# Two pairs of heads at a time in the gated attention layers of a fused model block

## The chip, the cores and the metric

One core of one Trainium2 chip runs the whole program as one launch. The metric is device time in microseconds (us). TensorE (PE in the rows) does matmuls and transposes, VectorE (DVE), ScalarE (ACT) and GpSimd (POOL) work on what it leaves in PSUM and SBUF, SyncE (SP) issues the weight loads. The granted TensorE clock was 1.000 of full speed (2.4 GHz) over the profiled execution.

## What is computed

The reference takes `x` of 512 tokens by 1024 in fp32 through four attention layers and then a mixed layer with a feed-forward part. The four layers are, in this order:

```
for i in range(DEPTH):                 # DEPTH = 4
    kind = i % 3
    y = _mla_branch(...) if kind == 0 else _swa_branch(...) if kind == 1 else _fox_branch(...)
    x = _layernorm(DEEPNORM_ALPHA * x + y, ln_g[i], ln_b[i])
```

Each has 16 heads with values of 64 columns and ends in `(o * silu(gate)) @ w_out`. In short:

- MLA (layers 0 and 3): latent queries (384) and keys and values (256), each head's query and key has 64 plain and 32 rotated columns, `softmax(q k^T * scale)` over all earlier keys, then times `v`.
- SWA (layer 1): 16 query heads over 4 key heads, a window of 128 keys, a slope times the distance subtracted from the scores, and a sink in the softmax's sum.
- FOX (layer 2): dense causal attention with `cum[q] - cum[k]` added to the scores, where `cum` is the running sum of the log of a forget gate.

The fifth layer is no gated attention: it joins a short convolution, a pooling mixer (means over 2, 4, 8, 16 tokens, each group times a matrix) and two attentions with a relative bias, one of them over selected keys; a feed-forward part of 2816 and a small gated embedding follow.

## The kernel before, in words

**Numbers.** Every fp32 matrix product is done as three fp32r matmuls: an operand is split in a high part (rounded to fp32r) and a low part (the rest), and the products high x high, high x low, low x high are added in PSUM (`three`, `columns`). ACT makes the high part, DVE (for weights GpSimd) the low part. Value products and transposes are plain fp32 matmuls.

**Weights** come in units of up to 128x1024 elements in the order of `plan_units`, which is also the order in which PE uses them. SP loads a unit into one of three raw buffers, ACT rounds it (`split`, three units ahead, called by `advance`), GpSimd makes the low part, and PE reads one of four places of a ring. A place comes free when PE is done with the unit in it.

**PSUM** has eight banks of 512 fp32 columns. Projections and value products ("groups") alternate between banks 6 and 7: PE waits for `bank_free` of the group before the last (`begin`), and the reader that takes a group's last part frees it (`stored`). Scores use banks 0 to 5 (0 to 3 in the window layer), transposed probabilities banks 4 and 5.

**A pair** is two heads that share a 128-row tile. `pair_attention` is written once for each of PE, ACT and DVE, and each is a list of steps in a fixed order; the semaphores tie the lists together. The steps for a pair are:

- PE `scores(i, ch)` (line 735; 748 with FOX's extra rows, 758 with the rotated part): 64-row matmuls, the two heads side by side. The 512 queries are taken in 128-query blocks t with 128 to 512 keys, put together in three chunks (two in SWA), each chunk in its own two banks.
- DVE `maxima(i, ch)` (L2274): adds mask or bias, writes the scores to SBUF (`SBP`, two buffers for even and odd pairs), takes the row maximum, and frees the chunk (`ps_free`). In SWA the bias of a pair is made first (L2265). After the last chunk come the negative maxima (L2284, L2286; semaphore `pnb`).
- ACT `exps(i, x)` for head x (L1551): the exponential in place, with its sum (`pexp`).
- DVE `norm(i, x)` (L2303): times the reciprocal of the sum (`pnorm`).
- PE `turn(i, x, ch)` (L776): 128x128 transposes, in chunks of up to four, three chunks a head (two in SWA), to a bank that ACT empties into `PTP` (`turned`, L1577, semaphore `pt_free`). A dense head has 10 transposes, a window head 7.
- PE `mix(i)` (L791): values times transposed probabilities, 64-column matmuls, the two heads side by side in one bank of the projections.
- DVE `mixed(i)` (L2318): times half the gate, into `otmp`; ACT `gated_high(i)` (L1601) rounds it, DVE `gated_low(i)` (L2327) makes the low part (semaphore `po_lo`). There is one `otmp`: a pair's product waits for the low part of the pair before it.

**The order before.** The loop runs i from -2 to 7. In each turn PE does the projections that later pairs need (`fill`) and weaves into them, every third matmul, the transposes of pair i; then it does all scores of pair i+2, then the value product of pair i. The last pair's transposes are woven into the first rows of the output projection (`out_ahead`). In MLA `fill` is a rope tile, a query tile, the keys and values of two pairs, and a gate; in SWA a query tile and a gate; in FOX a query tile, a key tile, a gate, and after every third pair the values (`pair_values`) of two pairs more. A query or key or gate tile of SWA and FOX is 24 matmuls of 512 columns. ACT's `fill` rounds the tiles, takes tanh of the gates, and issues small DMAs: `rel_rows` in SWA, `aug_rows` and `rope_tables` in FOX.

Two places outside the attention loops matter. Ahead of FOX, DVE sets constant rows (L2636 to L2645, eight of them of two rows each) and adds the forget bias (L2649, four small additions); ACT and DVE finish the log of the gate, and PE makes the running sum as matmuls (L1173). In the fifth layer, GpSimd makes the window sums (`window_sums`, L2875 to L2884) that PE multiplies in `pooled` (L1228).

## Time and profile before

| | us |
|---|---|
| median of 3 runs | 1663.32 (1662.29 to 1670.09) |
| the profiled execution | 1662.11 |
| its span, first to last instruction | 1660.1 |
| PE busy | 1630.5 (98%) |
| DVE busy | 777.2 (47%) |
| ACT busy | 768.8 (46%) |
| POOL busy | 653.8 (39%) |

Busy shares are shares of the span. A matmul's busy time begins when it starts and ends when its last column has left the array, so the next one starts while the last is still busy; what a matmul costs in a stream is the distance from its start to the next one's start. The idle time in brackets in the rows below is time in which the engine ran nothing, with the instruction that ended it.

### The profile page before, as it was taken

The numbers are of one execution on the slowest core, as the hardware profiler recorded it, in microseconds if no ns is written. First come the engines' busy times: TensorE is split into PE (matmuls) and PEld (weight loads), VectorE is DVE, ScalarE is ACT, GpSimd is POOL, SyncE is SP. The second block draws the span as 40 slices with busy tenths as digits, with TensorE's granted clock in tenths as the row PEclk, the third lists the DMA queues.
The fourth block names the chain that finished last, engine by engine and source line by source line (L and its number), as shares of the span: only waits on it lengthen the run. The fifth ranks groups of instructions, "written<-read, shape, count | busy, mean of one in ns | idle before, by whom it ended". The sixth has DMA issues, their size and how long they took to land.

```text
span 1660.1 us, 24632 instructions
## 1 busy us (share of the span) xinstructions
PE 1630.5 (98%) x9349; PEld 1334.3 (80%) x9349; DVE 777.2 (47%) x2048; ACT 768.8 (46%) x1565; POOL 653.8 (39%) x551
## 2 busy tenths in 40 slices
PE   8999999999999999999999999999999999999998
PEld 8777789887888787888787788777788888888877
DVE  3767635566453434445777646887151111001152
ACT  4466724656244545533567634428653323212252
POOL 5323234332343424235422244882235444444423
PEclk9999999999999999999999999999999999999999
DMA  6323144333542323144222156331243333333312
GB/s 174 71 46 79 47 165 132 79 72 69 156 135 77 90 53 95 58 165 107 61 66 58 52 179 183 92 89 52 84 145 102 96 95 102 101 90 94 123 63 89
DMA packets 216048, 161.19 MB, mean 97 GB/s; under 512 B 53755, under 2 KB 197147, under 8 KB 215932
## 3 DMA queue, kind: packets, MB, share of 16 engines
q1 hardware_dynamic: 205904, 130.21, 27.9%
q10 hardware_dynamic: 9804, 29.38, 5.9%
q8 instruction: 75, 1.23, 0.3%
q14 instruction: 41, 0.34, 0.1%
q0 software_dynamic: 224, 0.03, 0.1%
HBM read 148.32 MB, written 11.14 MB: 96 GB/s over the span
## 4 chain that ended last, share of the span: by engine, by line
PE 82%; DVE 9%; ACT 6%; issue 2%; POOL 1%; DMA 1%; DVEq 0%; SPq 0%; ACTq 0%; POOLq 0%
PE banks L543 40%; PE banks L494 8%; PE banks L496 7%; PE banks L495 7%; PE banks L776 5%; PE banks L791 4%; PE banks L735 4%; PE banks L625 4%; ACT AB L1551 2%; ACT w_hi L1421 1%; DVE banks L2414 1%; PE banks L758 1%; DVE banks L2403 1%; DVE AB L2416 1%; ACT G L1681 1%
## 5 line engine op out<-in xcount | busy, mean ns | idle before, releaser
L2920 POOL TENSOR_TENSOR w_lo<-w_raw,w_hi 128x512 fp32r<-128x512 f32 (+2 forms) x506 | 613.1, 1239 | 976.9 <-ACT w_hi L1421 965.6
L1421 ACT ACTIVATE w_hi<-w_raw 128x1024 fp32r<-128x1024 f32 (+4 forms) x254 | 249.2, 994 | 169.8 <-PE banks L496 103.0
L543 PE MATMUL banks<-XTh,w_hi 128*128 128x512 f32 (+5 forms) x1216 | 290.7, 375 | 3.8 <-DVE XTl L2376 1.4
L543 PE MATMUL banks<-XTl,w_hi 128*128 128x512 f32 (+5 forms) x1216 | 279.5, 368 | 0.0
L543 PE MATMUL banks<-XTh,w_lo 128*128 128x512 f32 (+5 forms) x1216 | 271.1, 365 | 0.0
L543 PEld LDWEIGHTS banks<-XTh,w_lo 128*128 128x128 f32 (+2 forms) x1216 | 211.0, 187 | 38.1
L543 PEld LDWEIGHTS banks<-XTh,w_hi 128*128 128x128 f32 (+2 forms) x1216 | 203.7, 188 | 43.6 <-issue 8.0
L543 PEld LDWEIGHTS banks<-XTl,w_hi 128*128 128x128 f32 (+2 forms) x1216 | 208.5, 187 | 35.4
L494 PE MATMUL banks<-w_hi,OTh 128*128 128x512 f32 (+1 forms) x448 | 172.7, 386 | 0.6 <-DVE QKl L2126 0.5
L496 PE MATMUL banks<-w_hi,OTl 128*128 128x512 f32 (+1 forms) x448 | 167.9, 375 | 0.0
L495 PE MATMUL banks<-w_lo,OTh 128*128 128x512 f32 (+1 forms) x448 | 167.9, 375 | 0.0
L1577 ACT ACTIVATE AB<-banks 128x512 f32<-128x512 f32 (+1 forms) x200 | 101.6, 529 | 140.0 <-PE banks L776 139.6
L1551 ACT ACTIVATE AB<-AB,nb 128x256 f32<-128x256 f32 (+3 forms) x288 | 152.5, 533 | 1.3 <-DVE nb L2286 1.2
L2303 DVE TENSOR_SCALAR_CACHE_REDUCE AB<-AB,ri 128x256 f32<-128x256 f32 (+3 forms) x256 | 118.2, 518 | 2.3
L2811 DVE TENSOR_TENSOR otmp<-banks,AB 128x512 f32<-128x512 f32 x22 | 15.2, 691 | 189.2 <-PE banks L543 189.2
L776 PE MATMUL banks<-ident,AB 128*128 128x128 f32 x672 | 100.7, 274 | 2.2 <-DVE mx L2274 1.1
L494 PEld LDWEIGHTS banks<-w_hi,OTh 128*128 128x128 f32 x448 | 84.3, 188 | 19.3 <-issue 2.4
L776 PEld LDWEIGHTS banks<-ident,AB 128*128 128x128 f32 x672 | 80.6, 140 | 23.6 <-issue 8.1
L2126 DVE TENSOR_TENSOR QKl<-banks,QKh 128x512 fp32r<-128x512 f32 (+2 forms) x80 | 54.6, 683 | 93.6 <-ACT QKh L1450 92.0
L496 PEld LDWEIGHTS banks<-w_hi,OTl 128*128 128x128 f32 x448 | 84.3, 188 | 15.4
L495 PEld LDWEIGHTS banks<-w_lo,OTh 128*128 128x128 f32 x448 | 84.5, 189 | 13.3
L2274 DVE CUSTOM_DVE_ANT_0 AB<-banks,zmask 128x256 f32<-128x256 f32 (+1 forms) x192 | 82.2, 485 | 0.4
(230 smaller groups left out, 2208.4 us busy)
## 6 DMA issues: line engine op xcount, KB each, us to landing
w_raw<-in_w_gate_up_dram SPq DMA_DIRECT2D x44, 512.0 KB, 3.8
w_raw<-in_fox_w_in_dram SPq DMA_DIRECT2D x30, 512.0 KB, 4.1
w_raw<-in_mla_w_in_dram SPq DMA_DIRECT2D x26, 512.0 KB, 5.0
w_raw<-in_w_in_dram SPq DMA_DIRECT2D x24, 512.0 KB, 3.9
w_raw<-in_w_down_dram SPq DMA_DIRECT2D x22, 512.0 KB, 3.5
w_raw<-in_swa_w_in_dram SPq DMA_DIRECT2D x20, 512.0 KB, 4.5
w_raw<-in_mla_w_out_dram SPq DMA_DIRECT2D x16, 512.0 KB, 3.9
x_spill<-AB ACTq DMA_DIRECT2D x16, 512.0 KB, 2.7
```

The lines of the kernel that those rows point to most:

```text
L494: nc.tensor.matmul(o, ah, bh, start=first, stop=False, skip_group_check=True)
L495: nc.tensor.matmul(o, ah, bl, start=False, stop=False, skip_group_check=True)
L496: return nc.tensor.matmul(o, al, bh, start=False, stop=last, skip_group_check=True)
L543: mm = nc.tensor.matmul(o, wt[:, k, :], xt[:, k, lo:hi], start=first and n == 0 and k == 0, stop=last and n == 2 and k == nk - 1, skip_gro ...
L625: mm = nc.tensor.matmul(o[:, 256 * (t % 2):256 * (t % 2) + 256], xt[:, k, ts], parts[k // 4][low][:, k % 4, :], start=n == 0 and k == 0, s ...
L776: mm = nc.tensor.transpose(bank[4 + c.tch % 2][:, o:o + P], SBP[a % 2][x][:, col:col + P], ident[:, :])
L1421: nc.scalar.activation(view(w_hi, u, RING), view(w_raw, u, RAW), ACT.Copy).then_inc(hi_done, 1)
L1551: ins = nc.scalar.activation(sc, sc, ACT.Exp, bias=nb[:, b, n0 + t:n0 + t + 1], scale=pr.scale, accum_out=rs[:, b, n0 + t:n0 + t + 1])
L1577: nc.scalar.activation(PTP[x][:, pr.pt[js[0]]:pr.pt[js[0]] + width], bank[4 + c.tch % 2][:, 0:width], ACT.Copy).then_inc(pt_free, 1)
L2274: ins = nc.vector.tensor_tensor_reduce(pr.score(b, x, t), o, pr.bias(t, x), 1.0, -3e38, ALU.add, ALU.max, mx[:, b, 4 * x + t:4 * x + t + 1])
L2303: ins = nc.vector.tensor_scalar(pr.score(b, x, t), pr.score(b, x, t), ri[:, b, 4 * x + t:4 * x + t + 1], None, ALU.mult, ALU.add, accum_ou ...
L2920: ins = pool.tensor_tensor(low[at], raw[at], high[at].bitcast(F32), ALU.subtract)
```

## The change

The four gated attention layers run two pairs at a time (`grouped`, which takes the place of `late`); the fifth layer's pairs keep their loop. For PE, a group s does: the projections for pairs 2s+2 and 2s+3 in one piece (`fill(s)`), all transposes of pairs 2s and 2s+1 (`block`), both value products, then all scores of pairs 2s+2 and 2s+3. Scores of pairs 0 and 1 come first. In the last group the transposes stay woven, two chunks at a time, into the first rows of the output projection (`last_block`, with `each=True` giving more points for it). Nothing is woven into projections any more.

```diff
+        TURN_BANKS = [4, 5, 0, 1, 2, 3]
+        def turn_bank(m, grouped, last):
+            return bank[TURN_BANKS[m % 6] if grouped and not last else 4 + m % 2]
+        def turned_to(pair, x, grouped):
+            return SBP[0][x] if grouped and pair % 2 else PTP[x]
...
+                def block(s):
+                    block_at[0] = c.tch
+                    pe.wait_ge(ps_free, s_first + s_len * (2 * s + 2))
+                    for i in (2 * s, 2 * s + 1):
+                        for x in range(2):
+                            for ch in range(len(pairs[i].t_chunks)):
+                                turn(i, x, ch)
...
+                def groups():
+                    fill(-1)
+                    for i in range(2):
+                        for ch in range(s_len):
+                            scores(i, ch)
+                    for s in range(n_pairs // 2):
+                        last = s == n_pairs // 2 - 1
+                        fill(s)
+                        if last:
+                            last_block(s)
+                        else:
+                            block(s)
+                        mix(2 * s)
+                        mix(2 * s + 1)
+                        if not last:
+                            for i in (2 * s + 2, 2 * s + 3):
+                                for ch in range(s_len):
+                                    scores(i, ch)
```

A block may fill six banks before the first must be empty (`held = 6`), since the scores' banks are read by then; the odd pair's transposed probabilities go to the even pair's score buffer. ACT and DVE get the lists that answer to it:

```diff
+                    # ScalarE, group s, i = 2 * s
+                        exps(i, 0)
+                        exps(i, 1)
+                        exps(i + 1, 0)
+                        fill(s, 0)
+                        exps(i + 1, 1)
+                        fill(s, 1)
+                        fill(s, 2)
+                        block_at[0] = c.tch
+                        turned(i)
+                        turned(i + 1)
+                        c.g += 2
+                        gated_high(i, c.g - 1)
+                        gated_high(i + 1, c.g)
...
+                    # VectorE, group s, i = 2 * s; maxima of pairs 0 and 1 come first
+                        fill(s, 0)
+                        norm(i, 0)
+                        fill(s, 1)
+                        norm(i, 1)
+                        fill(s, 2)
+                        norm(i + 1, 0)
+                        norm(i + 1, 1)
+                        fill(s, 3)
+                        mixed(i)
+                        gated_low(i)
+                        mixed(i + 1)
+                        for ch in range(s_len):
+                            maxima(i + 2, ch)
+                        gated_low(i + 1)
+                        for ch in range(s_len):
+                            maxima(i + 3, ch)
```

The projections of a group, on PE: in MLA rope(s+1), query(2s+2), a gate, keys(s+1), vals(s+1), query(2s+3), and for s = 0 a gate more; in SWA query, gate, query, gate; in FOX query, key, gate twice and then the values of two pairs. The last group has two gates. On ACT and DVE the `fill` steps of FOX are:

```diff
+                elif pos == 0:                      # ScalarE
+                    if s < 3:
+                        pair_tile((2 * s + 2) % 3)
+                        pair_tile(3 + (2 * s + 2) % 3)
+                elif pos == 1:
+                    advance()
+                    gate(2 * s)
+                else:
+                    if s < 3:
+                        pair_tile((2 * s + 3) % 3)
+                        pair_tile(3 + (2 * s + 3) % 3)
+                    if s < 2:
+                        act.wait_ge(ps_done, fox_s0 + 6 * (s + 1))
+                        aug_rows(s + 2)
+                        for n in range(2):
+                            rope_tables(1, 2 * s + n)
...
                     advance()
+                    gate(2 * s + 1)
+                    if s < 3:
+                        value_units((s + 1) % 2)
```

The weight units are put in the new order of use. FOX's and MLA's outputs go to other chunks of the output buffer (`FOX_OUT`, `MLA_OUT`, one MLA chunk in `QKh[:, 2]`) so that nothing is written over too early. Two steps outside the loops move:

```diff
@@ ahead of FOX, VectorE @@
+            c.g += 4
+            groups_stored(dve, c.g)
+            for t in range(T):
+                ins = nc.vector.tensor_tensor(FZ[...], FZ[...], bf[:, :], ALU.add)
+            ins.then_inc(fz_done, 1)
             for g in range(2):
                 for odd in range(2):
                     for x in range(2):
                         r0 = HD * x + ROPE * odd
                         nc.vector.memset(aug_k(g, odd)[r0:r0 + 2, :].bitcast(F32), 1.0).then_inc(fx_m, 1)
-            c.g += 4
-            groups_stored(dve, c.g)
-            ... (the four additions)
@@ the fifth layer, TensorE; ScalarE and VectorE move their steps with it @@
             pair_values(0)
-            pooled(1)
...
                 if pos == 0:
                     if i < 1:
                         pair_tile("q", i + 3)
+                        if i == -2:
+                            pooled(1)
```

## Rows read from the trace of the kernel before

**Rows 1.** The page, part 1: busy us, share of the span, instructions.
```profile
PE 1630.5 (98%) x9349; PEld 1334.3 (80%) x9349; DVE 777.2 (47%) x2048; ACT 768.8 (46%) x1565; POOL 653.8 (39%) x551
```

**Rows 2.** Busy us by engine in SWA, columns: stretch, length, PE, PEld, DVE, ACT, POOL.
```profile
303.00:423.00 120.00, 119.08 (x762) 95.31 (x761) 74.99 (x330) 72.90 (x210) 33.03 (x26) 1.00 0.34 67
```

**Rows 3.** PE in order of time (start, busy us), MLA, projection to scores.
```profile
122.54 0.39 PE L496 MATMUL banks<-OTh,w_lo 128*128 128x512 f32 x1
122.86 0.38 PE L735 MATMUL banks<-QKh 64*128 64x256 f32 x2
123.08 0.28 PE L735 MATMUL banks<-QKl,QKh 64*128 64x256 f32 x2
123.20 0.28 PE L735 MATMUL banks<-QKh,QKl 64*128 64x256 f32 x2
```

**Rows 4.** The same, scores to value product.
```profile
125.90 0.39 PE L758 MATMUL banks<-QKl 64*128 64x512 f32 x2
126.22 2.37 PE L791 MATMUL banks<-AB,V 128*64 128x512 f32 x16
```

**Rows 5.** The same, end of the value product to a projection.
```profile
128.20 0.39 PE L791 MATMUL banks<-AB,V 128*64 128x128 f32 x4
128.52 0.39 PE L494 MATMUL banks<-w_hi,OTh 128*128 128x256 f32 x1
128.74 0.28 PE L495 MATMUL banks<-w_lo,OTh 128*128 128x256 f32 x1
```

**Rows 6.** PE in SWA, transposes right after a value product.
```profile
341.03 0.99 PE L776 MATMUL banks<-ident,AB 128*128 128x128 f32 x7
341.77 0.94 PE L543 MATMUL banks<-XTh,w_hi 128*128 128x512 f32 x3
```

**Rows 7.** PE in MLA, transposes woven into a projection.
```profile
134.87 0.39 PE L543 MATMUL banks<-XTl,w_hi 128*128 128x512 f32 x1
135.10 0.60 PE L776 MATMUL banks<-ident,AB 128*128 128x128 f32 x4
135.45 0.94 PE L543 MATMUL banks<-XTl,w_hi 128*128 128x512 f32 x3
```

**Rows 8.** Waits of PE, whole span: total us, times, longest.
```profile
PE banks L1173 <- DVE QKl L2126: 1.5, 1, 1.5
PE banks L1228 <- POOL AB L2884: 1.3, 1, 1.3
PE banks L776 <- DVE mx L2274: 1.1, 2, 0.6
PE banks L543 <- DVE G L2159: 0.9, 1, 0.9
```

**Rows 9.** PE in SWA, first scores and first value matmuls of a turn.
```profile
353.68 0.33 PE L735 MATMUL banks<-QKh 64*128 64x128 f32 x2
...
355.29 1.08 PE L791 MATMUL banks<-AB,V 128*64 128x256 f32 x8
```

**Rows 10.** DVE in SWA: bias, end of chunk 0, gated product, negative maxima.
```profile
339.18 0.49 DVE L2265 TENSOR_SCALAR misc<-misc 128x256 f32<-128x256 f32 x2
...
340.82 0.08 DVE L2274 DVE_READ_ACCUMULATOR2_ANT mx<- 128x1 f32 x1
341.15 0.69 DVE L2318 SCALAR_TENSOR_TENSOR otmp<-banks,G 128x512 f32<-128x512 f32 x1 [0.25 <-PE banks L791]
...
343.25 0.36 DVE L2286 TENSOR_SCALAR nb<-mx,nsink 128x4 f32<-128x4 f32 x2
```

**Rows 11.** DVE in MLA, chunk 1 to the negative maxima.
```profile
131.57 0.55 DVE L2274 CUSTOM_DVE_ANT_0 AB<-banks,zmask 128x384 f32<-128x384 f32 x1
...
134.29 0.24 DVE L2284 TENSOR_SCALAR nb<-mx 128x4 f32<-128x4 f32 x2
```

**Rows 12.** ACT in MLA, two evictions of 512 columns.
```profile
132.19 1.08 ACT L1577 ACTIVATE AB<-banks 128x512 f32<-128x512 f32 x2
```

**Rows 13.** ACT's queue in FOX, one DMA issue of the augmented rows.
```profile
490.71 0.54 ACTq L1933 DMA_DIRECT2D QKh<-OTl  x1
```

More of the change, by code:

```diff
@@ L146, in plan_units @@
     tile("q", swa, P)
-    tile("gate", swa, D + 512)
-    tile("q", swa, 2 * P)
-    for i in range(1, 8):
-        if i + 2 < 8:
+    for i in range(8):
+        if i < 6:
             tile("q", swa, (i + 2) * P)
@@ L164, in plan_units @@
     fox_pair(1)
-    fox_pair(2)
-    for i in range(-1, 7):
-        if 0 <= i < 5:
-            fox_pair(i + 3)
-        tile("gate", fox, 3 * D + HEADS + (i + 1) * P)
-        if i in FOX_VALUES:
-            values(fox, 2 * D + 256 * FOX_VALUES[i])
+    for i in range(8):
+        if i < 6:
+            fox_pair(i + 2)
+        tile("gate", fox, 3 * D + HEADS + i * P)
+        if i % 2 and i < 6:
+            values(fox, 2 * D + 256 * (i // 2 + 1))
     rows("out", w["fox_w_out"][0], KD)
@@ L703, in pair_attention @@
                 s_first, s_len = c.sch, len(pairs[0].s_chunks)
-                at_end = pairs[0].late
-                shared = at_end and not pairs[0].window
+                grouped = pairs[0].grouped
+                block_at = [c.tch, False]
                 def scores(i, ch):
@@ L854, in pair_attention @@
                     fill(i, 2)
-                    if at_end and i < n_pairs - 1:
-                        woven.pop()
-                        while rest:
-                            next_turn()
-                        if i > -2:
-                            for ch in range(s_len):
-                                scores(i + 2, ch)
-                    elif not at_end:
-                        scores(i + 2, 2)
+                    scores(i + 2, 2)
                     mix(i)
@@ L1843, in fill @@
                         advance()
-                        gate(6 if i == 5 else (3, 4, 5, 7)[i // 2])
-                    elif pos == 2 and i < 6 and i % 2 == 0:
-                        query(i + 3)
+                        gate(5 + pos)
                 pair_attention(mla_pairs(), fill)
@@ L2336, in pair_attention @@
+                if grouped:
+                    groups()
+                else:
+                    for i in range(-2, n_pairs):
+                        fill(i, 0)
                         maxima(i + 2, 0)
                         maxima(i + 2, 1)
[L2338 to L2343 removed]
@@ L2780, in _ @@
             c.g += 2
-            pooled(1)
             dve.wait_ge(rel_in, 16 * 32)
```

600 lines of the change are left out of this document (284 added, 316 removed).

## The prediction

> **What bounds the kernel now.** I read the page's busy line first, then its chain of waits, then TensorE (PE) in order of time inside the three kinds of gated attention layer, and last VectorE (DVE) and ScalarE (ACT) there. The busy line gives PE 1630.5 us of 1660.1 [rows 1], and the chain that ended last runs through PE in nearly all of its length. In a stretch that covers sliding-window attention PE is busy 119.1 of 120 us, DVE 75.0, ACT 72.9 [rows 2]: nothing hides PE, and each nanosecond put into or taken out of PE's stream counts at full price. What the change can win is therefore (a) time that PE loses between matmuls of different kinds, and (b) the few real waits. What it can lose are new waits of PE for DVE or ACT, which have slack in the mean but now get their work in bursts. The profiled execution took 1662.11 us (span 1660.1); the median of the runs is 1663.32, 1.2 us more.
>
> **(a) Changes of array shape.** A projection is 128x128 fp32r matmuls ("M"), a score is pairs of 64-row matmuls ("R"), a value product pairs of 64-column ones in fp32 ("C"), a transpose an fp32 128x128 matmul ("T"). Steps are start to start.
> - M to R: the last M has 0.32 us to the first score, where a 512-column step is 0.23 [rows 7]; the first score pair then takes 0.22, the next of the same shape 0.12. Cost 0.09 + 0.10 = 0.19 [rows 3].
> - R to C: 0.32 instead of 0.23 for 512 columns, 0.09 [rows 4].
> - C to M: two pairs of 128 columns from 128.20 take 0.32 to the next M, though a product of 128 columns costs about 0.11, and the first M of 256 columns 0.22 instead of 0.12: 0.10 + 0.10 = 0.20 [rows 5]. R to M is taken as the same 0.20.
> - C to T: the same 0.10 on leaving, and seven transposes from 341.03 to the next M take 0.74, where four take 0.35 [rows 6, 7], so each further one 0.11 and three further 0.33: 0.06 more. Cost 0.16.
> - M to T and back: 0.01 a round trip by rows 7 (the M after a transpose starts early and then runs longer).
> By the Trainium skill, TensorEngine Tiling (Array Packing), Key Properties, changing the tiling mode, not just the tile, drains the engine; these rows agree, with 0.09 to 0.20 us a change.
>
> Before, one layer of eight pairs has: two visits to scores alone (scores of pairs 0 and 1), 2 x 0.39 = 0.78; six visits with scores and then a value product, 6 x 0.28 = 1.68, which leave to transposes five times and to projections twice over the seven products up to pair 6, about 1.2; M to C once 0.09; last product 0.30; some 32 woven round trips 0.3. Sum 4.4 us. After: one visit for the first two pairs 0.39; three groups of M to T, T to C, C to R, R to M; a last T to C, C to M and five woven trips 0.36. The trace has no undisturbed T to C and no C to R. T to C: nothing to 0.29 (the largest sum of one exit and one entry in rows 3 to 5), taken 0.10, as R to C. C to R: 0 to 0.30, taken 0.20, an exit of rows 5 with the entry of rows 3. So 0.39 + 3 x 0.51 + 0.36 = 2.3. Saved 2.1 to 2.2 a layer, four layers: **8.7 us** (5.5 to 12.5 by the bounds).
>
> **(b) Waits that go.** In MLA, PE stands before the transposes for a DVE maximum (1.1 in two waits), in SWA before a projection for a gate (0.9 in one); the memsets moved behind the bias addition free FOX's cumulative sum (1.5), and the second pooled matmul, moved behind a query tile, no longer meets GpSimd's window sums (1.3) [rows 8]. These numbers are idle only after the last matmul has run out of the array; a 512-column matmul is busy 0.39 and its step is 0.23 [rows 4, 7], so start to start each wait costs some 0.15 more. What is late next: DVE's four additions start about 3.4 us earlier, and the chain of ACT and DVE behind them with them, so the sum's operand is there when PE comes; a query tile of 24 matmuls at 0.23 (5.4 us) covers the window sums. 4.8 + 6 x 0.15 = **5.7 us** (bounds 3 to 6.5: the first two could reappear in new places).
>
> **(c) New waits of PE for DVE, at the scores of two pairs in a row.** All pairs use the same score banks, so each chunk of the second pair (B) waits until DVE has read that chunk of the first (A). Time 0 is the start of A's scores.
> *SWA.* PE needs 1.5 us for a pair (353.68 to 355.29, less the exit) [rows 9]. DVE: the gated product of the first pair ends its mixing at about -0.7; its low part waits for ACT's copy (0.6) and takes 0.6, to 0.55; the second gated product to 1.15; then bias and chunk 0 take 1.7 (339.18 to 340.9), to 2.85, and chunk 1 takes 1.4 (from the end of the gated product of 341.15, 0.6 later, to just before 343.25), to 4.25 [rows 10]. PE wants B's chunk 0 at 1.5 and gets it at 2.9: 1.4. It wants chunk 1 at 3.6 and gets it at 4.3: 0.7. So 2.1 a group, three groups, and 1.3 for the first two pairs, where DVE has no gated product ahead: **7.5 us**. Queued behind the waiting scores is all the rest of PE; nobody else waits.
> *MLA.* Five passes make a pair last 3.2 us (122.86 to 126.22 less the two changes) [rows 3, 4]. DVE's three chunks with the last bias take 3.7 (0.7, half of SWA's chunk 1; 1.4, 1.2 and the bias 0.3 from 131.57 to 134.5) [rows 10, 11]; A is done at 5.3, B's chunks are free at 1.7, 3.8 and 5.1, PE wants them at 3.3, 4.0 and 5.4: no wait. But DVE ends B only at 9.7, the rope tile's two readings (0.6 and 0.7, the length of the full-width rows in rows 10) free its bank at 11.0, and PE, after rope and query at 10.7, wants it: 0.3. With two small bank waits at the keys I take 0.5, twice a layer and two layers: **2.0 us**.
> *FOX.* Four passes, 2.6 us a pair: B's chunk 1 is wanted at 3.1 and free at 3.5, chunk 2 0.1 later than wanted: 0.5 four times, **2.0 us**.
>
> **(d) New wait of PE for ACT, at the transposes of two pairs in a row.** 40 transposes at 0.11 are 4.4 us, the first value product 2.2: the second wants the twelfth eviction 6.6 us after the block's start. ACT steps 0.5 a 512-wide eviction (two in 1.08 with the pipe's end) [rows 12] and an estimated 0.3, for half the width, for the four of 256: 5.2, after 0.6 for the copy of the last projection. 5.8 is 0.8 early, and the six banks let PE run ahead. Only in FOX a weight rounding of 1.0 stands between: 0.3 three times, **0.9 us**. SWA's chunks are smaller on both sides: 1.1 + 3.6 against 4.7, just even. Moved DMA issues cost ACT's queue about 0.5 each [rows 13]: six for the augmented rows and four for the rope tables now stand between a key tile and a gate, 5 us in which PE has a gate tile and two value halves to do (17 us), so nobody waits; if that cover were gone, the gate would come 5 us late, once a group. SP's queue has the same weight units in another order, GpSimd the same low parts. In MLA the rounding of the key-value weights waits behind three heads of exponentials (some 2.2 each, an estimate: four passes of the 0.5 in rows 12, with a short read behind each), to 12.9, GpSimd adds about 2.5, PE wants it at 16.5: no wait, cover 1.1. Normalised probabilities are ready at 17 and 24.6, PE transposes from 24 on.
>
> The last group keeps its woven form; its pairs' products come back to back, with over 10 us of output rows before their low parts are needed: nothing.
>
> **Sum.** -8.7 - 5.7 + 7.5 + 2.0 + 2.0 + 0.9 = -2.0 us. 1662.1 - 2.0 = 1660.1 for the profiled execution, 1661.3 against the median; I say **1660**. The terms' own bounds give -10 to +6.
>
> **Rivals.**
> 1. *The waits at the scores do not bind, or the unshown changes are free.* If DVE's maxima keep up (PE comes later than I count, or DVE's two gated products are quick), 7 to 9 of the 11.5 us under (c) are gone, and T to C and C to R at nothing add 3.8: -2 - 8 - 3.8, about 1649. For: DVE idles 45 us of the 120 in rows 2. Against: chunk durations and the order are fixed, and PE needs only 1.5 us a pair.
> 2. *The evictions come late.* Place: the second value product of each of the twelve blocks. ACT's twelve copies outrun by 0.8 us only; if each costs its full 0.6 instead of the 0.5 step (+1.2), or ACT is still in exponentials or a weight rounding (1.0), PE waits 1 us more in each block: +12, net +10, 1672. It decides from about 0.2 us a block beyond my cover, where the saving is used up. The Trainium skill, TensorEngine Tiling (Array Packing), PSUM Bottleneck, speaks for it: tiling speeds up the matmuls and not the PSUM evacuation, which may then be the bound, and both ScalarE and VectorE should evacuate. No row shows twelve evictions in a row.
> 3. *It does not do what it says:* all transposes together still give T to M no gain (0.01 a trip), so if the changes of shape were cheaper than I read (each drain partly hidden in the step I call extra), (a) gives 3 instead of 8.7 and the time is 1666, still inside half a per cent.
>
> **Chances.** Half a per cent (8.3 us) is about what a measurement of this kernel can tell from no change. Forecast with rival 3, 1655 to 1671: 0.52. Rival 1, below: 0.28. Rival 2, above: 0.20. Range 1649 to 1673: it takes in both rivals' centres and leaves out about 0.2. The forecast's own range is 1654 to 1668.
>
> **What would show it.** PE at L735's scores idle for DVE's maxima, about 2 us a group in SWA and none in MLA; the steps M to R halved in number; the second of two value products waiting for ACT only in FOX; no wait at the cumulative sum and at the second pooled matmul. Wrong would be an ACT wait over 0.5 us at every second product, or PE waiting for weights in the fills.

## The result, and the profile after

The changed kernel takes 1672.46 us (median of 13 runs, 1668.32 to 1683.44), the kernel before 1661.82 (13 runs beside them): ratio 1.0064, 95% interval 1.0052 to 1.0076. It is slower by 10.6 us, where 1660 was forecast, hardly a change at all. The time lies inside the range of 1649 to 1673, near its upper end. The kernel before is not free of slow executions either: 3 of its 79 runs, here and beside the experiments, took 1670.1 to 1670.3 us, two of them at a recorded clock of 0.994; no trace shows why.

The busy line of the page after, which answers to [rows 1]:
```profile
PE 1630.5 (98%) x9349; PEld 1348.0 (81%) x9349; DVE 786.6 (47%) x2048; ACT 765.4 (46%) x1565; POOL 661.8 (40%) x551
```
PE has as many matmuls and as much busy time as before; its span is 10.0 us longer (1670.1 against 1660.1). So the difference stands between the matmuls, or in matmuls that overlap less. I cut PE's time line of both profiled executions at the last output-row matmul of each layer, which gives the length of each layer ("after" is the changed kernel; the last column is a part of the fifth layer, so a row does not add up to the span):
```
us                  MLA 1    SWA     FOX    MLA 2   index, pool, mixed
before             196.09  202.27  290.32  245.63  235.69
after              196.71  211.73  289.31  246.33  235.98
```
9.5 of the 10.0 us are in SWA. The waits of PE over the whole span (total, times, longest) answer to [rows 8]:
```profile
PE banks L738 <- DVE mx L2320: 8.4, 8, 2.0
PE banks L497 <- DVE G L2205: 8.0, 8, 1.4
PE banks L497 <- DVE QKl L2172: 4.0, 5, 1.5
PE banks L779 <- ACT AB L1618: 0.7, 2, 0.4
PE banks L1264 <- issue: 0.6, 1, 0.6
```
The four waits of rows 8 are gone (the pooled matmul, now L1264, keeps 0.6 us of idle, but none for GpSimd). In their place stand the scores (L738) for DVE's maxima, as forecast, and the key and value tiles of MLA (L497) for DVE, which before was 3.8 in 4.

**The wait in SWA**, second group, PE and DVE in order of time (start, busy us, idle and releaser in brackets; some rows left out). A is the first pair of a group and B the second, as in the prediction:
```profile
329.54 0.69 DVE L2364 SCALAR_TENSOR_TENSOR otmp<-banks,G 128x512 f32<-128x512 f32 x1 [3.34 <-PE banks L794]
330.93 0.69 DVE L2373 TENSOR_TENSOR OTl<-otmp,OTh 128x512 fp32r<-128x512 f32 x1 [0.70 <-ACT OTh L1633]
330.93 0.33 PE L738 MATMUL banks<-QKh 64*128 64x128 f32 x2
331.75 0.69 DVE L2364 SCALAR_TENSOR_TENSOR otmp<-banks,G 128x512 f32<-128x512 f32 x1
332.32 0.28 PE L738 MATMUL banks<-QKh,QKl 64*128 64x256 f32 x2
332.36 0.49 DVE L2311 TENSOR_SCALAR misc<-misc 128x256 f32<-128x256 f32 x2
332.88 0.29 DVE L2320 CUSTOM_DVE_ANT_0 AB<-banks,misc 128x128 f32<-128x128 f32 x1
...
333.65 0.42 DVE L2320 CUSTOM_DVE_ANT_0 AB<-banks,misc 128x256 f32<-128x256 f32 x1
334.23 0.33 PE L738 MATMUL banks<-QKh 64*128 64x128 f32 x2 [1.63 <-DVE mx L2320]
...
334.67 0.58 PE L738 MATMUL banks<-QKh 64*128 64x256 f32 x2
334.99 0.47 PE L738 MATMUL banks<-QKl,QKh 64*128 64x256 f32 x2
335.21 0.47 PE L738 MATMUL banks<-QKh,QKl 64*128 64x256 f32 x2
```
A's scores last from 330.93 to 332.4. DVE is then just done with the second gated product (331.75 to 332.4), makes the bias, and reads A's chunk 0 only from 332.88 to 334.1; B's first matmul comes 1.9 us after A's last, where 0.12 is the step. The same step is 1.91, 1.91, 2.25 and 1.90 in the four groups. The first group has no gated product, and there another instruction stands ahead of the bias, the low part of the query tile that PE has just finished (A's scores start at 295.65):
```profile
296.48 0.69 DVE L2172 TENSOR_TENSOR QKl<-banks,QKh 128x512 fp32r<-128x512 f32 x1 [16.11 <-ACT QKh L1487]
297.09 0.48 DVE L2311 TENSOR_SCALAR misc<-misc 128x256 f32<-128x256 f32 x2
```

**The clock.** The last three rows are matmuls of 256 columns 0.22 to 0.3 us apart, where the same ones ahead of the wait stand 0.12 apart. The stretches of the profile say why (columns as in [rows 2]; the third from the right is the granted clock):
```profile
300.00:310.00 10.00, 9.76 (x44) 8.04 (x45) 6.50 (x36) 8.73 (x34) 2.23 (x2) 0.83 0.01 2
330.00:336.00 6.00, 4.37 (x52) 3.68 (x50) 5.10 (x24) 1.50 (x3) 0.00 (x0) 0.87 0.00 0
336.00:342.00 6.00, 6.00 (x32) 4.95 (x31) 5.59 (x31) 6.00 (x28) 0.00 (x0) 0.84 0.01 3
1014.00:1026.00 12.00, 11.02 (x84) 10.77 (x82) 7.62 (x12) 5.23 (x10) 0.16 (x1) 0.86 0.28 105
```
Up to 1650 us all other stretches are at 1.00, and so is every stretch of the kernel before. Right behind the first two of the score waits PE runs at 1.2 GHz for a while and then at 2.4 again. As an estimate, a stretch of length L at a mean clock k, with PE at work throughout, loses (1 - k) x L: 1.7, 0.8 and 1.0 in SWA, 1.7 in the index part, 5.2 in all. The mean over the span, 0.997, agrees (0.003 x 1670 = 5). The other runs go with it: 1668.32 us at a mean clock of 0.998, 1672.46 at 0.996, 1677.3 at 0.993, 1683.44 at 0.989; each is some 1665.3 plus the share lost, as near as a clock in thousandths can tell (0.8 us).

**The waits in MLA**, second group (some rows left out):
```profile
131.15 0.74 DVE L2349 TENSOR_SCALAR_CACHE_REDUCE AB<-AB,ri 128x512 f32<-128x512 f32 x1
131.82 0.68 DVE L2205 SCALAR_TENSOR_TENSOR G<-G,banks 128x512 f32<-128x512 f32 x1
132.35 0.52 ACT L1458 ACTIVATE w_hi<-w_raw 128x384 fp32r<-128x384 f32 x1 [1.37 <-DMA w_raw<-in_mla_w_q_up_dram]
132.55 0.50 PE L497 MATMUL banks<-OTh,w_hi 128*128 128x512 f32 x1 [0.84 <-DVE G L2205]
132.78 0.58 ACT L1487 ACTIVATE QKh<-banks 128x512 fp32r<-128x512 f32 x1
133.47 0.69 DVE L2172 TENSOR_TENSOR QKl<-banks,QKh 128x512 fp32r<-128x512 f32 x1 [0.97 <-ACT QKh L1487]
```
The second key tile needs the bank of the gate tile. ACT's half of the gate is ready from 131.0, but DVE first ends a normalisation (131.15) and reads the bank from 131.82 on; PE stands 0.84. The first key tile's bank is free only after ACT's copy and DVE's low part, and ACT's copy stands behind the rounding of a weight unit that waits 1.37 us for its DMA. Here the value half that follows just escapes; in the third group (2.13 us for the DMA) it waits 1.46.

### The profile page after: what moved, and what is told of

Same layout as the page of the kernel before. It is cut to its first block, busy times and chain, and to the rows that moved or that the text cites. A ratio compares the mean times of both kernels' runs of the same rounds, so it can differ in the third digit from the quotient of the medians.

```text
span 1670.1 us, 24551 instructions
## 1 busy us (share of the span) xinstructions
PE 1630.5 (98%) x9349; PEld 1348.0 (81%) x9349; DVE 786.6 (47%) x2048; ACT 765.4 (46%) x1565; POOL 661.8 (40%) x551
## 4 chain that ended last, share of the span: by engine, by line
PE 79%; DVE 10%; ACT 6%; issue 2%; DMA 1%; POOL 1%; ACTq 0%; SPq 0%; DVEq 0%
PE banks L546 40%; PE banks L497 7%; PE banks L499 7%; PE banks L498 7%; PE banks L779 5%; PE banks L794 4%; PE banks L628 4%; PE banks L738 3%; ACT AB L1589 2%; DVE AB L2320 2%; POOL w_lo L2975 1%; DVE banks L2466 1%; DVE banks L2455 1%; DVE AB L2468 1%; PE banks L1002 1%
## 5 line engine op out<-in xcount | busy, mean ns | idle before, releaser
L2975 POOL TENSOR_TENSOR w_lo<-w_raw,w_hi 128x512 fp32r<-128x512 f32 (+2 forms) x506 | 621.2, 1255 | 978.8 <-ACT w_hi L1458 967.5
L546 PE MATMUL banks<-XTh,w_hi 128*128 128x512 f32 (+5 forms) x1216 | 278.9, 372 | 2.5 <-DVE XTl L2428 1.4
L546 PE MATMUL banks<-XTh,w_lo 128*128 128x512 f32 (+5 forms) x1216 | 271.4, 366 | 0.0
L546 PE MATMUL banks<-XTl,w_hi 128*128 128x512 f32 (+5 forms) x1216 | 270.8, 365 | 0.0
L546 PEld LDWEIGHTS banks<-XTh,w_hi 128*128 128x128 f32 (+2 forms) x1216 | 209.4, 188 | 49.5 <-issue 8.8
L546 PEld LDWEIGHTS banks<-XTh,w_lo 128*128 128x128 f32 (+2 forms) x1216 | 211.6, 188 | 37.4
L546 PEld LDWEIGHTS banks<-XTl,w_hi 128*128 128x128 f32 (+2 forms) x1216 | 211.0, 187 | 37.7
L497 PE MATMUL banks<-w_hi,OTh 128*128 128x512 f32 (+1 forms) x432 | 165.9, 384 | 4.2 <-DVE QKl L2172 4.0
L499 PE MATMUL banks<-w_hi,OTl 128*128 128x512 f32 (+1 forms) x432 | 161.7, 374 | 0.0
L498 PE MATMUL banks<-w_lo,OTh 128*128 128x512 f32 (+1 forms) x432 | 161.4, 374 | 0.0
L1618 ACT ACTIVATE AB<-banks 128x512 f32<-128x512 f32 (+1 forms) x200 | 90.3, 567 | 35.5 <-PE banks L779 34.8
L2866 DVE TENSOR_TENSOR otmp<-banks,AB 128x512 f32<-128x512 f32 x22 | 15.2, 692 | 189.1 <-PE banks L546 189.1
L497 PEld LDWEIGHTS banks<-w_hi,OTh 128*128 128x128 f32 x432 | 81.3, 188 | 23.0 <-DVE QKl L2172 7.4
L1487 ACT ACTIVATE QKh<-banks 128x512 fp32r<-128x512 f32 (+2 forms) x80 | 46.6, 586 | 93.8 <-PE banks L546 75.0
L779 PE MATMUL banks<-ident,AB 128*128 128x128 f32 x672 | 83.8, 274 | 1.6 <-ACT AB L1618 0.7
```

The lines of the kernel that those rows point to most:

```text
L497: nc.tensor.matmul(o, ah, bh, start=first, stop=False, skip_group_check=True)
L498: nc.tensor.matmul(o, ah, bl, start=False, stop=False, skip_group_check=True)
L499: return nc.tensor.matmul(o, al, bh, start=False, stop=last, skip_group_check=True)
L546: mm = nc.tensor.matmul(o, wt[:, k, :], xt[:, k, lo:hi], start=first and n == 0 and k == 0, stop=last and n == 2 and k == nk - 1, skip_gro ...
L779: mm = nc.tensor.transpose(turn_bank(m, grouped, block_at[1])[:, o:o + P], SBP[a % 2][x][:, col:col + P], ident[:, :])
L1618: nc.scalar.activation(dst[:, pr.pt[js[0]]:pr.pt[js[0]] + width], src[:, 0:width], ACT.Copy).then_inc(pt_free, 1)
```

## The experiments

Theory 1: the forecast's own term (c) is the loss: PE's waits at the second pair's scores in SWA, and behind them the slower clock, which the forecast did not have. Theory 2: the loss lies elsewhere (MLA's banks, ACT's evictions). Theory 3: the clock has nothing to do with the waits. All twelve experiments at a glance (5 to 12 runs each, each beside runs of the kernel before); "clock" is the range over the runs of that kernel. A mean of 0.999 still leaves room for 1.7 us lost: the profiled e10_all_late stands at 0.999 and has a stretch at 0.88 from 1000 to 1014 (0.12 x 14):
```
run               us median  ratio to before (95%)      clock          SWA layer
after             1672.46    1.0064 (1.0052 to 1.0076)  0.989 - 0.998  211.73
e1_slots          1663.64    1.0008 (0.9999 to 1.0017)  0.999 - 1.000  203.64
e2_repeat         1669.84    1.0041 (1.0028 to 1.0054)  0.999 - 1.000  209.15
e3_two_moves      1660.50    0.9991 (0.9983 to 1.0000)  0.995 - 1.000  202.30
e4_keys_late      1674.66    1.0068 (1.0056 to 1.0080)  0.994 - 0.997  213.85
e5_gate_first     1670.96    1.0054 (1.0043 to 1.0066)  0.994 - 0.997  211.51
e6_in_place       1667.43    1.0033 (1.0022 to 1.0045)  0.999 - 1.000  206.47
e7_split_scores   1666.72    1.0028 (1.0017 to 1.0039)  0.994 - 1.000  208.43
e8_all            1661.43    0.9986 (0.9974 to 0.9998)  0.999 - 1.000  200.89
e9_keys_first     1665.11    1.0026 (1.0014 to 1.0039)  0.990 - 0.997  211.66
e10_all_late      1653.66    0.9944 (0.9931 to 0.9956)  0.999 - 1.000  200.94
e11_wait_again    1668.90    1.0042 (1.0029 to 1.0056)  0.993 - 0.996  213.64
e12_two_visits    1655.72    0.9958 (0.9946 to 0.9971)  0.999 - 1.000  200.90
```

### Other banks for the second pair
```diff
-self.s_banks = [0, 2] if self.window else [4, 0, 2]
+self.s_banks = ([4, 0] if gate % 2 else [0, 2]) if self.window else [4, 0, 2]
...
+elif pr.window:
+    pe.wait_ge(ps_free, c.sch - 2)
```


> The changed kernel, but in the sliding-window layer the four score chunks of a group rotate over three pairs of banks, so that the second pair's first chunk has banks of its own and waits for no maximum. Theory 1 (the second pair's waits at the scores, and the slower TensorE clock that follows them): PE's rows at L738 lose their 8.4 us of idle for DVE; the waits return start to start about 8 us and the mean granted clock goes back from 0.997 to 1.000, a further 2 to 5 us; 1672.5 becomes 1660 to 1663. Rival (the banks are not what holds PE, the maxima are late anyway, and the wait comes back at the second chunk or at the next projection): 1669 to 1673, idle at L738 or L546 of 6 us or more. Rival (the clock is no consequence of these waits): the clock stays at about 0.997 and the time at 1664 to 1666.

1663.64, 8.8 us less than the changed kernel, 0.6 above what theory 1 gave, and the clock is back. In the stretches where the changed kernel had 0.83, 0.87 and 0.84:
```profile
300.00:310.00 10.00, 10.00 (x53) 8.26 (x52) 7.39 (x42) 8.61 (x34) 1.31 (x2) 1.00 0.10 31
330.00:336.00 6.00, 5.15 (x47) 4.30 (x46) 5.90 (x33) 2.88 (x11) 0.00 (x0) 1.00 0.01 3
336.00:342.00 6.00, 6.00 (x28) 4.97 (x27) 4.07 (x23) 6.00 (x23) 0.96 (x1) 1.00 0.00 0
```
Theory 1 holds against both rivals of the forecast for this run. A part of the first rival shows, too: four waits of 0.64 to 1.20 us are left at the fourth chunk in SWA, because the maxima are late as well (the fifth in the row is FOX's):
```profile
PE banks L740 <- DVE mx L2322: 4.1, 5, 1.2
```

### The same wait, with PE at work
```diff
+if pr.window and i % 2 and ch == 0:      # ahead of the wait
+    ... the chunk's own matmuls, twice over, into bank[4 + x]
```


> The changed kernel with PE kept at work in the same wait: ahead of the wait for the second pair's first chunk, in each group of the sliding-window layer, PE computes that chunk twice over into the two unused banks (24 matmuls of the same form, about 1.9 us, thrown away). The wait for DVE stays where it is, only PE is not idle in it. If the slower clock follows from the idle time, the granted clock goes to 1.000 and the time falls by 3 to 6 us, to about 1667, though PE has more to do; if the clock loss has another cause, the time is 1672 to 1674 and the clock 0.997 as before; if PE's added work does not fit in the wait, up to 0.3 us a group is added.

1669.84 with the clock at 0.999 to 1.000 in all runs, though PE does 96 matmuls more; about 1667 was expected. The wait for DVE is in its place (what is left of it is 0.15 to 0.5 us in three groups), and the profiled execution has 1.00 throughout SWA. SWA takes 209.15, 2.6 less than in the changed kernel and not the whole 3.5 of the clock: that leaves 0.9 by which the added matmuls and their last stop (0.43 at the second chunk, where it was 0.33) overrun the old wait. So it is the idle array and not the waiting for DVE that brings 1.2 GHz.

### The wait put back into a fast kernel
The sharpest test came last; its kernel is the one of the last section on cures, e10_all_late.
```diff
 elif pr.window:
     pe.wait_ge(ps_free, c.sch - 2)
+    if i % 2 and ch == 0:
+        pe.wait_ge(ps_free, c.sch)
```


> The fastest kernel so far (1653.7) with one thing added: in the sliding-window layer PE waits ahead of the second pair's first chunk until both chunks of the first pair are read, though it has banks of its own. By that kernel's timeline this holds PE 2.3 us longer in the first group and 2.1 in each of the other three, 8.7 us in all, and no work changes. If idle time is all that such waits cost, 1662.4 at a granted clock of 0.999 to 1.000. If the slower clock follows from waits of this length, the clock falls below 0.998, 1.2 GHz shows in stretches right behind these waits, and the time is 1664 to 1672.

1668.90, 15.2 us more than e10_all_late. The added waits are 8.9 of it (idle 3.01, 2.31, 2.30 and 2.30 us against 0.63 and three of 0.14; 8.7 was worked out), and the other 6 go with the clock, 0.993 to 0.996 in every run. In the two profiled executions alone SWA is 12.7 longer, 3.8 beyond the waits. The stretches of the profiled one:
```profile
280.00:300.00 20.00, 16.99 (x124) 15.16 (x124) 6.58 (x36) 8.76 (x23) 5.03 (x4) 0.87 0.28 78
300.00:306.00 6.00, 6.00 (x25) 4.86 (x23) 2.64 (x16) 3.54 (x14) 2.03 (x2) 0.86 0.00 0
324.00:336.00 12.00, 9.69 (x95) 7.98 (x93) 6.95 (x35) 7.18 (x24) 0.00 (x0) 0.86 0.15 12
356.00:372.00 16.00, 13.70 (x127) 11.39 (x127) 8.95 (x44) 9.54 (x30) 0.33 (x1) 1.00 0.22 39
```
Two of the four waits are followed by 1.2 GHz, the third and fourth, as long, are not. Such chance would also explain how the clock varies from run to run, but only one execution of each kernel has a trace. Theory 3 falls.

The Trainium skill, TensorE: Matmul & The Clock Gate, A second HAM failure mode: psum-queue depth-cycling, describes a matmul kernel that cycles through PSUM banks and idles between groups often enough to make the clock oscillate, with the loss paid between the bursts. These runs agree in the kind of loss, but not in the pattern: here single waits of 1.6 to 3.0 us, over 30 us apart, are followed by it.

### DVE's order instead of the banks
```diff
-stored(nc.vector.scalar_tensor_tensor(otmp[:, :], o[:, :], 0.5, G[:, pr.gate, :], ...))
+stored(nc.vector.scalar_tensor_tensor(G[:, pr.gate, :], o[:, :], 0.5, G[:, pr.gate, :], ...))
...
 mixed(i)
-gated_low(i)
 mixed(i + 1)
 ... the first pair's maxima
+gated_low(i)
 gated_low(i + 1)
```


> The changed kernel with the score banks as they are, but DVE's queue shortened ahead of the maxima: the gated products are written over their gates, so that the second needs no low part of the first, and both low parts stand behind the first pair's maxima. DVE's first maximum of a group comes about 1.3 us earlier (0.7 for the low part, 0.6 for its wait on ACT's copy). If the order in DVE's queue sets PE's wait at the second pair's scores, that wait falls from 1.6 to 2.0 to about 0.4 us in three of the four groups (not in the first, which has no gated product ahead), 4 us, and a part of the slower clock goes with it: 1664 to 1667, with a granted clock of 1.00 after those three groups and below it after the first alone. If the reuse of the banks sets it whatever the order, 1671 to 1673.

1667.43. The three waits fall from 1.63, 1.98 and 1.63 to 0.93 each, not to 0.4: the first group's 1.64 stays. So banks and order each make a part of it. The clock is at 0.999 or 1.000 in all five runs, and the profiled one has 1.00 behind the 1.64 us too, against what was expected. And the new order costs: the low parts now stand ahead of DVE's reading of the rope tile, and PE waits 0.41 at MLA's gate tile in four groups.

### Room for DVE between the two pairs
```diff
 for i in (2 * s + 2, 2 * s + 3):
+    if i % 2 and pairs[0].window:
+        fill(s + 1, 0)          # the next query tile
     for ch in range(s_len):
         scores(i, ch)
```


> The changed kernel, but in the sliding-window layer the second pair's scores of the three later groups stand behind the next query tile, so that DVE has 5 us more; this costs a visit from projections to scores and back each time, 3 x 0.39 by the prediction's prices. If the waits were all of the loss, their three go (5.2 of idle, 5.9 start to start, and the slower clock after them), against 1.2 for the visits: 1672.5 - 5.9 + 1.2 - 2 to 3 = 1665 to 1666. If changes of array shape cost much more than read, it comes out at 1668 or above.

1666.72. The waits at the scores go in three groups, but PE stands 1.18 us in the query tile or the tile behind it instead. The one long wait at scores left is the first group's, 1.64. The clock is 0.998 to 1.000 in seven of eight runs and 0.994 in the other, the profiled one (1674.73 us). There a stretch at 0.84 stands right behind that wait, so one such wait can be enough; but most of the loss lies elsewhere, in the index part, where 1014 to 1026 is at 0.61 and 1026 to 1100 at 0.95, about 8 us (0.39 x 12 + 0.05 x 74).

### The two moved steps alone
```diff
 on the kernel before:
-memsets of aug_k; bias addition
+bias addition; memsets of aug_k
...
-pooled(1) ahead of the mixed layer
+pooled(1) behind its first query tile
```


> The kernel before with the two moved steps alone: the memsets of the augmented key rows behind the bias addition, and the second pooled matmul behind a query tile. The prediction's step (b) gives 1.5 + 1.3 + 2 x 0.15 = 3.1 us less than before, 1658.7 against 1661.8; if they only move their wait elsewhere, 1661.8. No slower clock is expected in it by any theory.

1660.50, 1.9 us less by medians taken side by side (1662.38), where 3.1 was expected. Its FOX layer takes 288.81 instead of 290.32, 1.5 as worked out; the pooled matmul's wait is gone. But the profiled execution has a stretch at 0.88 from 1000 to 1014, nearly the same place as the changed kernel's last stretch at 0.86, and one of the twelve runs stands at 0.995 (1666.67 us). No theory had a slower clock here. So the 1.7 us there belong to single executions of either kernel and not to the grouping.

### The latent layers: three orders
Values ahead of keys:
```diff
-keys(s + 1); vals(s + 1)
+vals(s + 1); keys(s + 1)        # on PE, ACT and DVE
```


> The changed kernel with the values of a key-value weight unit computed ahead of its keys in the three later groups of each latent layer, so that the second key tile's bank was last read by ACT and not by DVE's gate, which stands in DVE's queue behind a normalisation. If the key-bank waits cost what their start-to-start steps say (six of about 1.0 us and four at the first value tile of 0.3 to 1.6), the time falls by 6 to 9 us, to 1664 to 1667, and PE's idle at L497 behind DVE falls from 12 us to 5 or less. If the sliding-window layer and the clock are all of the loss and these waits only take the place of later ones, it falls by less than 2 us, and a wait of like size shows at the next query tile or the transposes.

1674.66: nothing won. A value half is 12 matmuls at 0.12, 1.4 us, as short as a key tile at six of 0.23; the tile two behind the gate meets the same unread bank (PE at L497 behind the gate still 7.7 us in 8 waits). I had taken it for longer. The 2.2 us more than the changed kernel go with the clock of 0.994 to 0.997.

Gate ahead of a normalisation, key copies ahead of a rounding:
```diff
 # ScalarE
-advance()
 hi(...); hi(...)
+advance()
 # VectorE
 query(2 * s + 2); rope_sum()
+gate(MLA_GATE[s])
 norm(i, 1)
-gate(MLA_GATE[s])
 keys()
```


> The changed kernel with two orders mended in the three later groups of each latent layer: DVE applies the gate before the normalisation of the pair's second head instead of behind it, and ACT copies the two key tiles before it rounds the next weight unit instead of behind it (there it stood 1.4 and 2.1 us for the unit's DMA). Theory: the two waits of PE in these fills, between the two key tiles (0.84 to 0.96, six times) and between keys and values (0.4 to 1.5, five times), come from these two queues; they go but for 0.1 to 0.2 us each, 7 to 9 us in all, and the time falls to 1663.5 to 1666. Rival: PE overtakes in a place with nothing to spare and meets the same engines at the next tile; less than 3 us are won, and a wait shows at L779 or the query tile.

1670.96, and 195.89 and 245.42 us for the two latent layers: 1.7 won, as the rival had it. The first wait fell to 0.1 to 0.4, and each group then had 1.02 at the value half:
```profile
130.34 0.69 DVE L2208 SCALAR_TENSOR_TENSOR G<-G,banks 128x512 f32<-128x512 f32 x1 [1.23 <-ACT G L1521]
132.35 0.74 DVE L2352 TENSOR_SCALAR_CACHE_REDUCE AB<-AB,ri 128x512 f32<-128x512 f32 x1
133.02 1.28 DVE L2175 TENSOR_TENSOR QKl<-banks,QKh 128x512 fp32r<-128x512 f32 x2
133.76 0.39 PE L497 MATMUL banks<-w_hi,OTh 128*128 128x256 f32 x1 [1.02 <-DVE QKl L2175]
```
The normalisation (to 133.0) had only changed its victim: both low parts of the keys stand behind it. So they go ahead of it as well:
```diff
 gate(MLA_GATE[s])
+keys()
 norm(i, 1)
-keys()
```


> The changed kernel with the latent layers' fills mended once more: DVE takes the gate and then both key tiles' low parts before the normalisation of the pair's second head (in the run before this one only the gate, and PE then stood 1.02 at the first value half in each group, behind that normalisation). By the timeline of that run the low parts are done at about 132.3 and 133.7, when PE wants their banks at 132.5 and 133.9, and three normalisations of 2.1 follow before the transposes of the second pair's second head at 141. Theory: both waits go in all six groups, 4.8 + 5.0 start to start less 0.1 to 0.2 each, so that each latent layer takes 192 to 193.5 (first) and 242 to 243 (second) where it was 196.7 and 246.3; the time falls 6 to 8 us, to 1664 to 1666. Rival, as before: the wait moves on, now to the transposes for the normalisations; less than 3 us are won.

1665.11; the layers take 193.31 and 242.77, 7.0 us less than in the changed kernel, the middle of what was expected. The normalisations are in time for the transposes. SWA is untouched, 211.66, and the clock with it (0.990 to 0.997). So theory 2 holds beside theory 1, for MLA's banks: they cost about as much as the slower clock does.

### The cures together


> The three cures together: score banks that rotate in the sliding-window layer, gated products in place, and the two orders of the latent layers. From the run with rotating banks, 1663.6: less 7 to 9 for the latent layers, less about 2.9 for what is left of waits at the fourth score chunk in three groups: 1652 to 1654, granted clock 1.000, about 9 us below the kernel before. If the gains do not add (the freed engines meet another bound, weight supply above all), 1656 to 1660.

Rotating banks, products in place, and the order of e5_gate_first: 1661.43, since the latent layers' wait only moved on (196.95 and 246.44). That misses the forecast of 1652 to 1654 by the 8 us that were put on the latent layers, and lies above the rival's 1656 to 1660, too. Then with the order of e9_keys_first, and both low parts behind the next group's maxima and the rope tile:
```diff
 fill(s, 0)
+if s:
+    gated_low(i - 2); gated_low(i - 1)
 norm(i, 0)
 ...
 mixed(i); mixed(i + 1)
-gated_low(i); gated_low(i + 1) among the maxima
```


> Rotating banks in the sliding-window layer, gated products in place with both low parts moved behind the next group's maxima (and behind the rope tile's readings), and the latent layers' order of the run beside it. From the run with all cures so far, 1661.4 (latent layers 196.95 and 246.44, with a new wait of 0.41 at the gate tile in four groups, the low parts standing ahead of the rope tile): less 3.5 to 4.5 in each latent layer, the sliding-window layer as it was at 200.9: 1652 to 1655, 7 to 10 us below the kernel before, at a granted clock of 1.000. If the latent layers' waits only move on, 1658 to 1661.

1653.66, ratio 0.9944 (0.9931 to 0.9956): 8.6 us below the kernel before and 18.8 below the changed one. The layers take 193.21, 200.94, 289.30 and 242.68; the gains add. Its waits at the scores, all layers:
```profile
PE banks L740 <- DVE mx L2325: 1.2, 2, 0.6
```

### What a visit costs
```diff
 in two groups of FOX, on e10_all_late:
 for i in (2 * s + 2, 2 * s + 3):
+    if i % 2 and s < 2: fill(s + 1, 0)     # the next query tile
     scores(i, ...)
```


> The fastest kernel so far (1653.7) with two changes of array shape more in each of two groups of the forgetting layer: the second pair's scores stand behind the next query tile, so that PE goes to projections and back to scores once more. No wait hangs on it (the small ones for the maxima, 0.3 in all, go). By the prediction's prices each visit costs 0.20 on leaving and 0.19 on coming: 2 x 0.39 - 0.3 = +0.5 us in that layer, 289.8 instead of 289.3, and 0.78 over its four changes of shape. If each change cost as little as rival 3 had it, a third of that, the layer is unchanged or shorter, 289.2.

1655.72 in all, 2.1 more; FOX takes 291.82, 2.52 more, which neither theory expected. Of it 2.27 are two new waits, for a weight unit that ACT rounds behind exponentials:
```profile
571.00 1.17 PE L546 MATMUL banks<-XTh,w_hi 128*128 128x512 f32 x4 [0.97 <-ACT w_hi L1468]
```
(a step of 1.36 instead of 0.23, twice), and 0.34 of small waits went. That leaves 2.52 - 2.27 + 0.34 = 0.6 for two visits, 0.30 each, against 0.39 of the forecast and 0.13 of rival 3.

## Why the prediction was wrong

Step by step, in the profiled executions (us; the measured column from steps start to start). For (a) it is what is left of each layer's difference when its waits and clock are taken out, so the sum closes by construction and is no check of (a):
```
step                               predicted   measured
(a) changes of array shape            -8.7       -7.2   (MLA -2.0 and -2.3, SWA -1.9, FOX -1.0)
(b) waits that go                     -5.7       -5.3   and 1.3 of small waits for weights and banks
(c) SWA, waits at the scores          +7.5       +8.9
(c) MLA, new waits                    +2.0       +7.8
(c) FOX, waits at the scores          +2.0       +1.5
(d) evictions                         +0.9       +0.6
    slower clock                        0        +5.2
sum                                   -2.0      +10.2   (the spans: +10.0)
```
The forecast missed by 12.2 us (+10.2 against -2.0). The largest parts are the fills of MLA (5.8) and the slower clock (5.2, of which 3.5 in SWA); then (a) 1.5 and SWA's waits 1.4, against 1.7 the other way in the rest.
- **(a)** right in kind, somewhat dear. T to C and C to R, not shown before, can be read now (the first row covers two products):
```profile
562.69 4.53 PE L794 MATMUL banks<-AB,V 128*64 128x512 f32 x32
567.15 0.39 PE L738 MATMUL banks<-QKh 64*128 64x256 f32 x2
567.37 0.28 PE L738 MATMUL banks<-QKl,QKh 64*128 64x256 f32 x2
567.49 0.29 PE L738 MATMUL banks<-QKh,QKl 64*128 64x256 f32 x2
```
A product's last pair has 0.20 to the first scores and these 0.22 to the next, where 0.12 and 0.12 are the plain steps: C to R costs 0.2, as taken; T to C, 0.20 instead of 0.11 and 0.47 instead of 0.42 at the first product step, 0.14 where 0.10 was taken. The whole visit costs 0.30 by e12_two_visits.
- **(b)** right: FOX's sum by e3_two_moves, and the last column of the layer table is 1.4 shorter when the clock's 1.7 is taken out.
- **(c), SWA**: the place, the cause and the count (B's first chunk, DVE's queue, four groups) were right, and e1_slots took them away. The chunk 0 term was 1.4 a group and measured 1.8 to 2.1: counted from A's first score, the second gated product ends at 1.5 where 1.15 was forecast, and PE gets chunk 0's bank at 3.3 instead of 2.85; one group is 0.35 later still. Chunk 1 cost 0.5 in three groups instead of 0.7. Most of the difference is the first group, put at 1.3 because no gated product stands there, which cost 2.3: the forecast had left out the low part of the query tile, which ends 1.5 after A's first score, as late as the gated product does elsewhere. But the first step that failed the forecast is a term it had put at nothing without a reason: **the wait was priced at its own length**. e11_wait_again shows what waits of this kind bring with them, 6 us of slower clock for 8.9 of waiting by the medians, and e2_repeat shows that it is the idle PE.
- **(c), MLA**: the second step that failed, and the larger one in the profiled executions: 2.0 was forecast and 7.8 measured. The wait was looked for at the rope tile's bank (0.3, it doesn't wait there: no idle at L546 or L497 ahead of the gate) and "two small bank waits at the keys" were put at 0.2. It was just these that grew: the second key tile waits 0.84 to 0.97 in all six groups (before, 0.57 in the first group of each layer, with 0.98 at the first key tile), a value half 0.4 to 1.5 in five, about 3.7 and 4.1 us a layer more than before. Grouping puts the gate's reading behind a normalisation on DVE, and a weight rounding that waits for its DMA in front of ACT's key copies; I had counted DVE's work at the scores instruction by instruction, and not in the fill. e9_keys_first took 7.0 back.
- **(d)** right: three stops of 0.19 among the transposes of FOX, none in SWA or MLA. Rival 2, whose 1672 is by chance the time that came, is wrong in its mechanism: PE waits for ACT at the products no more than before, so that the forecast's range took in the measured time by luck. Rival 1 is wrong on the waits, and rival 3 on the prices.

So without the slower clock the change would cost about 3.5 to 5 us, an estimate (the runs extrapolate to 1665.3 against 1661.8; the steps give 5.0). It would still be slower where 2.0 less was forecast, through MLA's fills most of all; with it 10.6. The grouping itself is worth having once the queues behind it are put in order (e10_all_late).

Left open: why one wait of 1.6 to 2.3 us is followed by 1.2 GHz and the next is not, and the slow stretch that starts between 1000 and 1026 us, which eight of fourteen profiled executions have, one of them of a kernel without grouped layers (e3_two_moves). In the changed kernel it stands behind a wait of 0.98 us for DVE (at 1018.5, the longest of the three in this row), which e1_slots and the kernel before have there as well, without a slow stretch:
```profile
PE banks L546 <- DVE XTl L2428: 1.4, 3, 1.0
```

## What to carry to other kernels

When two like stages are put back to back on the bound engine, the waits between them are not only their own length: count every reader of a reused bank in the other engines' queues, in the fills as well as in the stage that was moved, and look at the granted clock behind each wait of a microsecond or two. If an engine overtakes, mend the whole queue that it meets: one instruction moved ahead of a normalisation only handed the wait to the next tile, two moved took 7 us back. Moving a tile between other tiles did not help here, because it was as short as the one it replaced, and the chain that frees the bank was longer than either (e4_keys_late).

## What the runs showed of the hardware

- The clock fell to 1.2 GHz behind single waits of 1.6 to 3.0 us in front of 64-row score matmuls, in some executions and not in others; in no run's trace did it fall in these places behind waits of 0.6 to 1.2 us (e1_slots, e6_in_place behind its last three, e8_all, e10_all_late). In the changed kernel waits of 1.3 to 1.5 us in MLA had no such effect, and those of the kernel before at 61, 483 and 799 us (1.3, 1.5 and 1.4) neither. With 24 short matmuls put into each wait the clock stayed at 2.4 GHz in SWA (e2_repeat). Long waits at the scores are not all: single executions of kernels with and without grouped layers had 1.2 GHz in the index part, from 1000 us on.
- ACT's twelve evictions in a row take 5.13 us (MLA, from 140.00), where 5.2 was worked out from the 0.5 of [rows 12] for eight wide ones and 0.3 for the four narrow ones.
